# Seven-product pairs in a float32 FFN: two weight sums by an accumulating DMA, two part sums added in PSUM, two low parts in one operation, some signs turned

## The reference, cut to what matters

```python
def swiglu(x, w_gate, w_up, w_down):
    return (jax.nn.silu(x @ w_gate) * (x @ w_up)) @ w_down
# layer l:
x = x + 0.5 * swiglu(rmsnorm(x, norm_w[l, 0]), ffn_w_gate[l, 0], ffn_w_up[l, 0], ffn_w_down[l, 0])
x = x + mixer(rmsnorm(x, norm_w[l, 1]))          # mLSTM in layer 0, gated linear attention in layer 1
x = x + 0.5 * swiglu(rmsnorm(x, norm_w[l, 2]), ffn_w_gate[l, 1], ffn_w_up[l, 1], ffn_w_down[l, 1])
```

## Time and profile before

| | |
|---|---|
| median of 3 runs (lowest to highest) | 2196.25 us (2194.16 to 2197.27) |
| profiled execution, span from first to last instruction | 2198.8 us |
| PE busy | 2160.5 us, 98% |
| DVE busy | 1555.5 us, 71% |
| ACT busy | 951.1 us, 43% |
| POOL busy | 45.7 us, 2% |
| DMA, mean share of 16 engines | 28.1% on the SP queue, 92 GB/s |

### The profile page before, as it was taken

The page is one execution under the profiler, slowest core; times in us unless marked ns, Lnnn a source line. Parts: engine busy times, 40 slices in busy tenths (PEclk is TensorE's granted clock), DMA queues, the critical chain, the costliest instruction groups (busy, mean ns, idle before and its releaser), DMA issues.

```text
span 2198.8 us, 40702 instructions
## 1 busy us (share of the span) xinstructions
PE 2160.5 (98%) x16360; PEld 2137.4 (97%) x16360; DVE 1555.5 (71%) x2379; ACT 951.1 (43%) x1495; POOL 45.7 (2%) x50
## 2 busy tenths in 40 slices
PE   7999999999999999999999999999999999999997
PEld 7999999999999999999999999999999899999997
DVE  6898657685555798848679984863776457988485
ACT  5435435454433444515445452544322434445252
POOL 0000000001100000000000000000011100000000
PEclk9999999999999999999999999999999999999999
DMA  5222322224332232222323232232122222223222
GB/s 186 68 88 95 115 67 86 96 82 137 99 118 85 68 102 82 95 87 89 104 70 94 86 96 96 82 101 94 44 96 84 97 77 84 90 87 104 77 86 73
DMA packets 72578, 201.58 MB, mean 92 GB/s; under 512 B 7268, under 2 KB 26980, under 8 KB 72448
## 3 DMA queue, kind: packets, MB, share of 16 engines
q1 hardware_dynamic: 72448, 199.80, 28.1%
HBM read 187.82 MB, written 11.95 MB: 91 GB/s over the span
## 4 chain that ended last, share of the span: by engine, by line
PE 91%; DVE 5%; ACT 2%; issue 1%; DMA 0%; POOL 0%; SPq 0%; DVEq 0%; POOLq 0%
PE ps L479 48%; PE ps L536 32%; PE ps L753 4%; PE ps L608 1%; DVE w_lo L1768 1%; PE ps L784 1%; PE ps L773 1%; PE ps L787 0%; DVE w_lo L1753 0%; PE ps L803 0%; PE ps L617 0%; PE ps L796 0%; PE ps L631 0%; PE ps L797 0%; DMA x<-in_x 0%
## 5 line engine op out<-in xcount | busy, mean ns | idle before, releaser
L479 PE MATMUL ps<-h_lo,w_hi 128*128 128x288 f32 x1616 | 347.0, 294 | 4.1 <-DVE h_hi L2267 4.1
L479 PE MATMUL ps<-h_hi,w_hi 128*128 128x288 f32 x1616 | 346.5, 294 | 0.7 <-DVE w_lo L1753 0.7
L536 PE MATMUL ps<-th_hi,w_hi 128*128 128x288 f32 x1088 | 320.2, 294 | 2.4 <-ACT scratch L1219 2.4
L536 PE MATMUL ps<-th_lo,w_hi 128*128 128x288 f32 x1088 | 320.9, 295 | 0.0
L536 PE MATMUL ps<-th_hi,w_lo 128*128 128x288 f32 x1088 | 319.8, 294 | 0.0
L479 PE MATMUL ps<-h_hi,w_lo 128*128 128x288 f32 x1360 | 290.2, 292 | 0.0
L479 PE MATMUL ps<-xn_hi,w_hi 128*128 128x288 f32 x1152 | 257.2, 300 | 11.6 <-DVE w_lo L1753 8.9
L479 PEld LDWEIGHTS ps<-h_lo,w_hi 128*128 128x128 f32 x1616 | 259.9, 188 | 4.8 <-DVE h_hi L2267 4.5
L479 PEld LDWEIGHTS ps<-h_hi,w_hi 128*128 128x128 f32 x1616 | 259.9, 188 | 1.0 <-DVE w_lo L1753 0.9
L1753 DVE TENSOR_TENSOR w_lo<-raw,w_hi 128x1024 fp32r<-128x1024 f32 x196 | 232.2, 1221 | 36.9 <-ACT w_hi L1185 35.1
L479 PE MATMUL ps<-xn_hi,w_lo 128*128 128x288 f32 x1152 | 251.9, 296 | 0.0
(11 more groups left out here) (288 smaller groups left out, 4119.7 us busy)
## 6 DMA issues: line engine op xcount, KB each, us to landing
raw<-in_w_gate SPq DMA_DIRECT2D x88, 512.0 KB, 3.4
raw<-in_w_up SPq DMA_DIRECT2D x88, 512.0 KB, 4.2
raw<-in_w_down SPq DMA_DIRECT2D x64, 512.0 KB, 3.6
raw<-in_w_mix SPq DMA_DIRECT2D x64, 512.0 KB, 4.2
raw<-in_w_down SPq DMA_DIRECT2D x32, 384.0 KB, 3.2
state_s<-in_state_c SPq DMA_DIRECT2D x4, 1024.0 KB, 7.5
out_c_s<-state_s SPq DMA_DIRECT2D x4, 1024.0 KB, 4.6
state_s<-in_state_g SPq DMA_DIRECT2D x4, 1024.0 KB, 6.1
```

The lines of the kernel that those rows point to most:

```text
L479: ins = nc.tensor.matmul(o, a, b[:, c] if c is not None else b, start=first and j == 0, stop=last and j == 2)
L536: ins = nc.tensor.matmul(ps[:, bank, FIRST], left, b_, start=first and k == 0 and j == 0, stop=k == KT_X // 2 - 1 and j == 2, skip_group_c ...
```

## The change

- **Host and loads.** w_gate and w_up are laid out together as `w_gu`: for each block W12, W11, W21, W22, 512 columns each. Slot 0 of a half takes W12 and W11, slot 1 takes W21 and W22. `raw` has one row for each half, with room between the two slots: the upper 512 columns of that room, next to slot 1, take a second copy of W11 (`s3_start`, 256 KB, on SP's queue right behind the load of slot 1). The buffer `bc` of the mixers, formerly one of its own, lies in that room too.
- **Two sums by DMA.** When slot 1 and the copy are full, POOL issues one DMA that adds W21 and W22 (512 KB from HBM) to the adjacent 1024 columns that hold W11 and W21. This gives S3 = W11 + W21 and S1 = W21 + W22 in place. DVE and ACT wait for it on `sums_full`.
- **The other two by DVE.** S2 = S1 + W11 and S4 = W12 + S2, into two buffers each.
- **Signs.** The sums above differ in sign from the scheme before, so the signs of some token sums are turned (`u_sums`, `t_sums`), up comes out negative, and x takes -0.5 times the down product.
- **Merged parts.** High and low part of W11 and W12 are one operation of 1024 columns each (`weights_high`, `weights_low`). P1 is copied from PSUM to PSUM, and the part sums U2 and U4 are written back into PSUM banks, so that further products accumulate there; of four `part` additions two are left.
- **Orders.** PE: W11, S3, S2, W12, S1, W22, S4, and W22 also waits for the first part sum (`part_ready`). DVE: `sum_2` of the next pair now stands at the head of `seven_pair`, ahead of `rows_product`. ACT: `weights_high` and `sums_high` of the next pair each come one step earlier.

```diff
 def load(ph, i, s, first=False):
     n = 2 * ph["base"] + 4 * i + s
     if not first:
         sp.wait_ge(lo_done, n - 3)
-    sp.dma_start(raw[:, s, 0:ph["k"] * P],
+    sp.dma_start(raw_slot(s, ph["k"] * P),
                  block_source(ph, i, s).rearrange("o p n -> p (o n)")).then_inc(raw_full[s], 16)
+
+def s3_start(ph, i, half):
+    if ph["group"] == 0:
+        sp.wait_ge(rstd_ready, ph["norm"] + 1)
+    m = ph["ffn"] * (D_FF // P) + ph["k0"] + 2 * i + half
+    sp.dma_start(raw_unit(half, S3_AT),
+                 io["w_gu"][bass.ds(m, 1), :, UNIT:2 * UNIT].rearrange("o p n -> p (o n)"))\
+        .then_inc(s3_full[half], 16)
...
+def weight_sums(ffn):
+    for ph in PHASES:
+        if ph["kind"] != "G" or ph["ffn"] != ffn:
+            continue
+        for m in range(ph["skip"], ph["pairs"]):
+            i, half, pair = m // 2, m % 2, ph["base"] + m
+            pool.wait_ge(raw_full[2 * half + 1], 8 * (pair - half) + 16)
+            pool.wait_ge(s3_full[half], sums_at(ph, i, half))
+            G.dma_start(raw[:, half, S3_AT:S1_AT + UNIT], io["w_gu"][ffn * (D_FF // P) + ph["k0"] + m, :,
+                                                                    2 * UNIT:4 * UNIT],
+                        accum_op=ALU.add).then_inc(sums_full[half], 16)
...
+def sum_2(ph, i, half):
+    pair = ph["base"] + 2 * i + half
+    dve.wait_ge(raw_full[2 * half], 8 * (pair - half) + 16)
+    dve.wait_ge(sums_full[half], sums_at(ph, i, half))
+    V.tensor_tensor(s2(half), raw_unit(half, S1_AT), raw_unit(half, W11_AT), ALU.add).then_inc(sum_ready, 1)
...
 def seven_pair(j, ph, i, half, before, last):
     if before and ph["group"] == 0:
         rows_scale(ph, *before)
     if not last:
-        dve.wait_ge(unit_lo, 5 * w + 3)
-        sum_3(ph, *after)
+        sum_2(ph, *after)
     if before:
         rows_product(ph, *before)
-    dve.wait_ge(sum_ready, 4 * w + 4)
-    dve.wait_ge(unit_hi, 5 * w + 4)
-    unit_low(half, 0, by_tile(S1)).then_inc(unit_lo, 1)
+    if not last:
+        sum_4(ph, *after)
+    dve.wait_ge(unit_hi, 4 * w + 3)
+    unit_low(half, U_S1, raw_unit(half, S1_AT)).then_inc(unit_lo, 1)
     if before:
         rows_low(ph, *before)
     dve.wait_ge(hi_done, 2 * pair + 2)
-    unit_low(half, 1, raw_tiles(half, 1, 1)).then_inc(lo_done, 1)
-    dve.wait_ge(copy_done, 3 * w + 1)
+    unit_low(half, U_W22, raw_unit(half, W22_AT)).then_inc(lo_done, 1)
+    if not last:
+        weights_low(ph, *after)
+    dve.wait_ge(copy_done, 3 * w + 2)
     dve.wait_ge(product_done, 6 * w + 2)
-    part(T(0)[:, FIRST], half, 0, P1_COPY)
-    dve.wait_ge(unit_hi, 5 * w + 5)
-    unit_low(half, 2, by_tile(S4)).then_inc(unit_lo, 1)
...
+    V.tensor_tensor(ps[:, b + 2, FIRST], ps[:, b + 3, FIRST], U2_COPY, ALU.add).then_inc(part_ready, 1)
+    dve.wait_ge(unit_hi, 4 * w + 4)
+    unit_low(half, U_S4, s4(half)).then_inc(unit_lo, 1)
     if last:
         split(PHASES[j + 1], 0, 0, (0,))
     else:
         sums_low(ph, *after)
-    dve.wait_ge(product_done, 6 * w + 6)
-    dve.wait_ge(part_ready, 4 * w + 2)
-    part(T(1)[:, FIRST], half, 3, T(4)[:, SECOND])
+    dve.wait_ge(copy_done, 3 * w + 3)
+    V.tensor_tensor(ps[:, b + 3, FIRST], ps[:, b + 3, FIRST], U4_COPY, ALU.add).then_inc(part_ready, 1)
...
-pe.wait_ge(unit_lo, 5 * w + 1)
-product(0, b + 1, x_tiles(even, 0), True).then_inc(product_done, 1)
 pe.wait_ge(lo_done, 2 * pair + 1)
-product(1, b, x_tiles(odd, 0), True).then_inc(product_done, 1)
-pe.wait_ge(unit_lo, 5 * w + 2)
+product(U_W11, b + 1, x_tiles(even, 0), True).then_inc(product_done, 1)
+pe.wait_ge(unit_lo, 4 * w + 1)
+product(U_S3, b + 3, t_tiles(2), True).then_inc(product_done, 1)
+pe.wait_ge(unit_lo, 4 * w + 2)
 pe.wait_ge(copy_done, 3 * w + 1)
-product(2, b + 1, t_tiles(1), False).then_inc(product_done, 1)
-pe.wait_ge(unit_lo, 5 * w + 3)
-product(3, b + 2, t_tiles(2), True).then_inc(product_done, 1)
-pe.wait_ge(unit_lo, 5 * w + 4)
+product(U_S2, b + 1, t_tiles(1), False).then_inc(product_done, 1)
+product(U_W12, b, x_tiles(odd, 0), False).then_inc(product_done, 1)
+pe.wait_ge(unit_lo, 4 * w + 3)
 pe.wait_ge(copy_done, 3 * w + 2)
-product(0, b + 1, t_tiles(0), False).then_inc(product_done, 1)
+product(U_S1, b + 1, t_tiles(0), False).then_inc(product_done, 1)
 pe.wait_ge(lo_done, 2 * pair + 2)
-product(1, b + 3, t_tiles(3), True).then_inc(product_done, 1)
-pe.wait_ge(unit_lo, 5 * w + 5)
+pe.wait_ge(part_ready, 2 * w + 1)
+product(U_W22, b + 2, t_tiles(3), False).then_inc(product_done, 1)
+pe.wait_ge(unit_lo, 4 * w + 4)
 pe.wait_ge(copy_done, 3 * w + 3)
-return product(2, b + 1, x_tiles(odd, 1), False)
+return product(U_S4, b + 1, x_tiles(odd, 1), False)
```

More of the change, by code:

```diff
@@ L32 @@
 SSQ_LAST = 4 * (N_NORMS - 1)
+SEVEN_FROM = 5
 def schedule():
-    out, pair, hidden, seven = [], 0, 0, 0
+    out, pair, hidden, seven, by_half = [], 0, 0, 0, [0, 0]
     for layer in range(2):
@@ L47, in schedule @@
             for g, (k0, k) in enumerate(GROUPS):
+                skip = 0 if g else SEVEN_FROM
+                skipped = [(skip + 1 - half) // 2 for half in range(2)]
                 out.append(dict(kind="G", pairs=k, base=pair, ffn=ffn, norm=norm, k=KT_X, k0=k0,
-                                group=g, hidden=hidden, seven=seven - (0 if g else 5), plain=5 * ffn,
-                                scaled=3 * ffn - 5))
-                pair, hidden, seven = pair + k, hidden + k, seven + (k if g else k - 5)
+                                group=g, hidden=hidden, seven=seven - skip, plain=SEVEN_FROM * ffn,
+                                scaled=(GROUPS[0][1] - SEVEN_FROM) * ffn - SEVEN_FROM, skip=skip,
+                                by_half=[by_half[half] - skipped[half] for half in range(2)]))
+                pair, hidden, seven = pair + k, hidden + k, seven + k - skip
+                by_half = [by_half[half] + k // 2 - skipped[half] for half in range(2)]
                 out.append(dict(kind="D", pairs=4, base=pair, ffn=ffn, norm=norm, k=k, k0=k0,
@@ L460, in _ @@
                     continue
-                with sp.Fori(1 if j == 0 else 0, ph["pairs"] // 2) as i:
-                    for s in range(4):
-                        load(ph, i, s)
+                if ph["kind"] == "G" and ph["group"] == 0:
+                    for m in range(2 if j == 0 else 0, ph["pairs"]):
+                        for blk in range(2):
+                            load(ph, m // 2, 2 * (m % 2) + blk)
+                        if m >= SEVEN_FROM:
+                            s3_start(ph, m // 2, m % 2)
+                    continue
+                with sp.Fori(0, ph["pairs"] // 2) as i:
+                    for half in range(2):
+                        for blk in range(2):
+                            load(ph, i, 2 * half + blk)
+                        if ph["kind"] == "G":
+                            s3_start(ph, i, half)
             for c in range(2):
@@ L1184, in split @@
                     act.wait_ge(raw_full[slot], 8 * (pair - half) + 16)
-                    nc.scalar.activation(w_hi[:, slot, :], raw[:, slot, :], ACT.Copy).then_inc(hi_done, 1)
+                    nc.scalar.activation(w_hi[:, slot, :], raw_slot(slot), ACT.Copy).then_inc(hi_done, 1)
             def split_next(j, i, half):
@@ L1198, in unit_high @@
             def unit_high(half, u, src):
-                return nc.scalar.activation(by_tile(unit(w_hi, half, u)), src, ACT.Copy)
+                return nc.scalar.activation(unit(w_hi, half, u), src, ACT.Copy)
             def weights_high(ph, i, half):
@@ L1242, in seven_rest @@
                     split(PHASES[j + 1], 0, 0)
-                else:
-                    sums_high(ph, *step(i, half))
             def seven_rows(ph, i, half, last):
                 m = 2 * i + half
-                w, pair, q = ph["seven"] + m, ph["base"] + m, ph["hidden"] + m
+                w, pair, b = ph["seven"] + m, ph["base"] + m, 4 * half
                 if ph["group"]:
-                    act.wait_ge(part_ready, 4 * w + 1)
-                    nc.scalar.activation(T(0)[:, FIRST], T(0)[:, FIRST], ACT.Silu)
                     act.wait_ge(pe_done, pair + 1)
-                    nc.scalar.activation(T(0)[:, SECOND], ps[:, 4 * half + 1, FIRST], ACT.Silu).then_inc(gate_done, 1)
+                    nc.scalar.activation(cut2(T(0)), ps[:, b:b + 2, FIRST], ACT.Silu).then_inc(gate_done, 1)
                 else:
@@ L1651, in late_split @@
                         act.wait_ge(raw_full[slot], 8 * (base + 2) + 16)
-                        nc.scalar.activation(late_weights(xn_hi, pp, blk, n), raw[:, slot, 0:n], ACT.Copy)\
+                        nc.scalar.activation(late_weights(xn_hi, pp, blk, n), raw_slot(slot, n), ACT.Copy)\
                             .then_inc(hi_done, 1)
@@ L1842, in seven_pair @@
             def seven_pair(j, ph, i, half, before, last):
-                pair, w = ph["base"] + 2 * i + half, ph["seven"] + 2 * i + half
+                pair, w, b = ph["base"] + 2 * i + half, ph["seven"] + 2 * i + half, 4 * half
```

(9 more changed lines are left out.)

187 lines of the change are left out of this document (98 added, 89 removed).

## The result

| | before | after |
|---|---|---|
| median | 2196.75 us (2194.16 to 2197.27) | 2376.66 us (2368.71 to 2383.69) |
| ratio | | 1.0821, 95% interval 1.0795 to 1.0846 |
| span of the profiled execution | 2198.8 us | 2366.9 us |

8.2% slower; 2364 us was forecast. The medians lie 179.9 us apart, the two profiled executions 168.1: the one after is the fastest of its four runs, and the one before lies 2 us above its median. So the traces account for 168 us, and the other 12 have no trace. The runs after also lie further apart, 15 us against 3.

What follows compares the result with a forecast made beforehand. PE bounds the kernel, but a new DMA loop would set the pace: G1 22.8 + G2 14.6 + G0 5.1 = 42.5 us an FFN, 170 for four, less 2.4: +168 on 2196.25, 2364 us; range 2218 to 2491.

Steps and rivals of the forecast that it cites:

- PE-bound, so relief on DVE and ACT is worth little: Whole kernel: PE busy 98%; work off DVE and ACT gains nothing in G1 and G2, at most 2.4 us in G0.
- the loop: Seven-product pairs: slot 1 freed, loads, POOL's DMA, sum_2, DVE's queue to W22's low part; 8.4 + A, 15.2 us a pair.
- A: Time of POOL's 512 KB accumulating DMA in each pair's round: taken as 6.8 us, bounds 3.3 and 9.5.
- estimate of 4.4: Alternative for POOL's DMA time from the skill pages: 2.0 + 2.4 us, the change then costing 62 us, 2258.
- What reaches the end: Lateness left after PE's 1.8 us of room: G1 22.8, G2 14.6, G0 5.1 us, 42.5 for an FFN.
- the forecast's own rule: G1 costs 6d - 1.8 and G2 4d - 1.8 us, d being the round's excess over PE's pace, forecast 4.1.
- rival of a clock that stays low: G stages: PE's clock stays at the lower level, 22.2 us a pair, some +755, 2950 us; chance 0.03.
- D stages unchanged: Profile after: the D stages were expected to stay as before, while G1 and G2 grow.
- Hidden: Rival: POOL's DMA under 3.0 us, loop keeps PE's pace; 2198 us, or 2194 if all 2.4 are won; chance 0.08.
- slightly late: Rival: POOL's DMA near the plain load, 3 to 4 us; 2210 to 2240 us; chance 0.14.
- much slower: Rival: POOL's DMA over 9.5 us from slow element-wise adding; over +286, over 2482 us; chance 0.07.

Runs made afterwards that it cites:

- no DMA: Kernel after without POOL's accumulating DMA, its waiters waiting for the loads of slot 1 and the copy, S3 and S1 not summed: 2209.06 us, ratio 1.0055.
- sums later: Kernel after with DVE's sum_2 and sum_4 behind W22's low part and weights_low behind the first part sum, all DMAs kept: 2208.23 us, ratio 1.0056.
- the last experiment: Kernel after with DVE's sums moved later, plus most D-stage blocks ordered one PSUM bank after the other: 2204.94 us, ratio 1.0034.

## Why the prediction was right, point by point

**PE-bound, so relief on DVE and ACT is worth little: right.** DVE lost 141 us (I had 160), and where the loop was cut, G0 gained 0.7 us (no DMA) and 1.1 (sums later), and G1 nothing: it lost 0.1 and 0.9.

**The loop: right in its links, wrong in the size of two,** and shown by cutting it in two different ways. Its terms, for the round from 924.48:

| term | forecast | measured |
|---|---|---|
| loads of slot 1 and copy | 4.4 | 4.25 (to 928.73) |
| landing to POOL's issue (forecast with DVE's wake-up) | 0.15 | 0.54 (to 929.27) |
| A, issue to landing | 6.8 | 5.42 (to 934.69) |
| DVE from `sum_2` to the end of W22's low part | 3.83 | 3.87 (to 938.56) |
| SP | 0.03 | 0.15 (to 938.71) |
| round | 15.2 | 14.2 (mean of five 14.47) |

The term that was mis-sized is A, 1.4 us too high: I took the loads of 1024 KB in the trace as nearest by bytes. The 1024 KB in 5.5 us of the earlier trace rows would have been right to 0.1. The Trainium skill's fit ("DMA: Bandwidth & Descriptors", Anatomy of one DMA), from which the prediction worked out its estimate of 4.4 with the bytes counted twice, was too low by 1.0; for the plain copy it would give 2.0 + 1.2 = 3.2, an estimate again, and 3.7 was measured. The second term off is the hand-over: over the five rounds landing to POOL's issue has a mean of 0.59 us and DVE to SP 0.16, 0.57 more than forecast, against the 1.3 that A (mean 5.47) is shorter. So the round is 14.47 and not 15.2, 3.4 us over PE's pace and not 4.1.

**What reaches the end: near in sum, in part by luck.** G1 was to cost 22.8 and costs 21.0 here, G2 14.6 and 12.1, G0 5.1 and 5.0. With the measured round the forecast's own rule would have given 18.4 for this G1 and 11.7 for G2. One error is what PE waits for. I had S1's low part and U2's sum. It is the copy of U2, which ACT makes behind the high part of the rows, of W22 and of the next weights:

```profile
936.20 0.69 ACT L1320 ACTIVATE h_hi<-scratch 128x576 f32 x1 [2.59 <-DVE scratch L1893]
936.79 0.62 ACT L1261 ACTIVATE w_hi<-raw 128x512 fp32r<-128x512 f32 x1
937.31 1.04 ACT L1268 ACTIVATE w_hi<-raw 128x1024 fp32r<-128x1024 f32 x1
938.25 0.39 ACT L1280 ACTIVATE scratch<-ps 128x288 f32<-128x288 f32 x1
```

These are ACT's operations in the same round; PE's fifth product starts at 938.70, behind the last of them. I had followed only DVE's queue behind `rows_product`, not ACT's. It takes some 0.2 us more of PE's room than U2's sum would. PE stands still 13.9 us in this G1, 2.3 a pair and not the 4 of the forecast: its matmuls, slower behind each gap, fill the rest (95.94 us busy against 88.80). The other error is the end of a group. PE's last ten products, three of the last pair but one and all seven of the last, start after a gap of 3.65 us and wait for nothing more:

```profile
982.79:985.00 2.21, 2.21 (x9) 2.21 (x10) 2.21 (x4) 1.50 (x3) 0.00 (x0) 0.50 0.44 104
985.00:990.00 5.00, 5.00 (x36) 5.00 (x35) 1.40 (x3) 1.01 (x2) 0.00 (x0) 0.88 0.43 166
```

The granted clock is at the lower level, 1.2 GHz, for all of the first 2.21 us and (0.88 as the mean) for about a quarter of the next 5. Within the group that fits into the waiting, as forecast; here these 120 matmuls take 17.70 us, where PE's pace gives 15.86. Other ends differ; the chain has for the ends of G0, G1 and G2 in this FFN, and of G1 in the next:

```profile
821.84 17.65 PE ps L597 x120
982.79 17.70 PE ps L597 x120
1114.16 16.17 PE ps L597 x120
1416.93 18.94 PE ps L597 x120
```

At 1114.16 the gap ahead was nearly as long (3.4 us), and the clock stayed at 1.00. All twelve ends of groups together took 21.5 us more than at PE's pace, and the forecast had nothing for them. That G0 comes out at 5.0 against 5.1 is luck: 1.8 of it are this clock. The rival of a clock that stays low did not come: 0.94 as the mean of this G1.

**The D stages: not foreseen.** 12 stages by 1.27 us are 15 of the 168 us between the spans. The forecast's "D stages unchanged" is wrong.

**The sum.** A round of 14.47 in place of 15.2 makes the forecast's 168 some 32 us less (A alone 59 less, the hand-overs 25 more), D 15 more and the ends of the groups 21.5 more: 172, where the spans differ by 168. So the mechanism was right, and that the sum came within 1% is luck: the mis-sized A is made up for by two terms that the forecast put at nothing.

**The rivals.** Hidden, slightly late, much slower and low clock are all out with A at 5.4 and a granted clock of 0.94 in G1; A would have had to be under 3.0 to be hidden, and even a plain copy from POOL takes 3.7.

## What to carry to other kernels

Ask of each new wait not only when its data come, but whether the waiting instruction stands in its queue ahead of the one that lets the next transfer start; if it does, latency becomes a pace, and each microsecond costs as often as the loop runs. The mend is one of order: what frees a buffer goes ahead of what waits for the next one, here worth 168 us with the DMA left as it is. Follow every queue behind a late step, ACT's as well as DVE's, and look up what clock was granted behind a gap, above all where no later wait absorbs it (here 0.3 to 3.1 us each time).

## What the runs showed of the hardware

- A DMA of POOL that adds 512 KB from HBM into SBUF lands 5.4 us after its issue, one of 256 KB after 3.7, a plain one of 512 KB after 3.7. So adding the second 256 KB costs 1.7 us, as much as adding costs over copying. With this DMA left in and `sum_2` moved, the matmuls ran at their pace (11.10 us a pair) at 0.5 to 0.7 of the DMA engines.
- From the landing of the data that POOL waits for to POOL's issue 0.5 to 0.7 us passed; from the end of a DVE operation to SP's issue about 0.16 in the kernel after.
- The same matmuls alternating between two PSUM banks ran at 130.0 or at 133.3 ns each over whole stages, without any wait, at the full clock. Bank by bank they ran at about 132. Both gaits occur in one kernel and even in one stage (the last experiment's D1: 132.9, then 130.0 behind blocks ordered by bank).
- After PE stood still for 3.65 us, its clock was granted at 0.50 for 2.21 us and at 0.88 for the next 5; after another gap, of 3.4 us, it stayed at 1.00.
